# Two-block transformer kernel: paired value products, tanh gates, modulation chunks one a turn

## The chip, the cores and the metric

The kernel runs on one core of a Trainium2 chip, as one launch. The time is the device time of that core in microseconds (us). All of the work is in float32 or in pairs of rounded float32r parts. TensorE (PE) does the matrix products, VectorE (DVE) and ScalarE (ACT) the elementwise work, GpSimd (POOL) helps with weights, and SyncE (SP) issues the weight transfers.

## The reference

The reference is two transformer blocks after each other on 256 tokens of width 1024, each two layers deep. The change touches three places of it. In block one, attention is a mix of small attentions; the modulation rows of block two are computed beside it:

```
mod  = silu(c)     @ w_ada[l] + b_ada[l]
modc = silu(c_ctx) @ w_ada[l] + b_ada[l]        # 9 x 1024 values each
```

In block two, eight heads attend to 512 keys (256 context and 256 latent tokens), and three branches are merged through gates:

```
s = einsum('bqhd,bkhd->bhqk', q, k) * ATTN_SCALE
p = softmax(s, axis=-1)
o = einsum('bhqk,bkhd->bqhd', p, v)             # V_DIM = 64 a head
g = sigmoid(u @ w_bg + b_bg)                    # 3 x 1024 gates
y = (g0 * y_conv + g1 * y_mla + g2 * y_four) @ w_out
```

## The kernel before, in words

The program is written by hand: each engine has one instruction list, and the engines meet at semaphores. Nothing is reordered, so the order of the work is the order of the code.

**The weight stream.** All weights come as chunks of at most 128x1024 float32 (512 KB) through a ring of four slots. SP issues chunk n as soon as chunk n-4 has been used. For most products a chunk is split into a rounded high part (L771 on ACT) and the rest (L795 on DVE, L2361 and L2363 on POOL), and PE makes three passes (L834, L838, L841).

**Block one's attention** (`attention_pe`, `attention_act`, `attention_dve`) walks over 22 units a layer in 24 turns. In turn n PE does the scores of unit n+1 (L1100, L1108 or L1111, with masks at L1117), then the modulation chunks due in this turn (`ada_pe`, L932), then the transposes of unit n-1 (L1126 or L1129), then the values of unit n-2 (L1142, L1148), then a modulation fold if one is due (`ada_fold_pe`, L913). DVE takes the maximum (L1187), normalizes (L1210 to L1218) and adds the bias to folded rows (`ada_dve`, L953). ACT does the exponentials (L1240), the copies and the drain of the modulation bank (`ada_act`, L943). The first 11 units read 128 keys, the last 11 read 256.

**Modulation chunks.** `ADA_TICKS` says how many of a layer's 20 chunks are multiplied in each of 28 ticks; the first four ticks lie ahead of the attention, tick 4 + n is turn n. A chunk is two products of 32 output rows each; the chunks with an even number write rows 0 to 63 of the bank, the others rows 64 to 127. After 12 and after 20 chunks a bank is complete: ACT drains it one tick later, PE folds it two ticks later, DVE adds the bias three ticks later.

**Block two's attention** (`units_block2`) has in layer zero 16 units of one head with 512 keys and then 8 units of two heads with 256 keys; in layer one the 16 units of one head alone. In turn i PE does group i of the conv and fourier branch products (L834, L838, L841 for the gate, L2346, L2349, L2352 for the branch; turns 0 to 15 only), the scores of unit i+1 (L2003), the transposes of unit i-1 (L2012) and the values of unit i-2 (L2023). ACT does the exponential of unit i (L2055), the next weight split (L771), the gate (L2435), the copy of the transposes of unit i-1 (L2062) and the copy of the values of unit i-2 (L2067). The probabilities, `pt`, have two buffers by the parity of the unit. The value product of one head gives 64 of the 128 output rows of `bank7`: rows 0 to 63 for an even head, 64 to 127 for an odd one. A layer-zero branch turn of DVE also computes modulation rows (L962, L964).

**Tables.** The exponential of L2055 and the sigmoid of L2435 lie in different table sets of ScalarE, and an ACT_TABLE_LOAD stands ahead of each of them in turns 0 to 15; L2656 loads the sigmoid's set for the third branch.

## Time and profile before

| what | us |
|---|---|
| median of 3 runs | 2862.97 (2861.08 to 2864.32) |
| the profiled execution, its own time | 2866.21 |
| its span in the trace | 2864.4 |
| PE busy in the span | 2767.5 (97%) |
| DVE, ACT, POOL busy | 1779.1, 1124.7, 187.0 |

The trace is of one execution. Its own time is 1.8 us more than its span and 3.2 us more than the median. A busy engine here is one that has an instruction in flight; PE's instructions overlap, so the time of a row of PE work is best read from the start of one row to the start of the next.

### The profile page before, as it was taken

The page shows a single profiled execution, that of the slowest core. Times are in us where ns is not written, and L with a number is a line of the kernel's source. Part 1 is how long each engine was busy: PE and PEld are TensorE (multiplying, and loading weights), DVE is VectorE, ACT ScalarE, POOL GpSimd, SP SyncE. Part 2 cuts the span into 40 slices and gives each one's busy share as a digit, 9 for nine tenths or more (in the row PEclk, how much of TensorE's full clock was granted, in tenths as well). Part 3 has the DMA queues.
Part 4 walks back from the last instruction along what each step waited for, and adds up shares of the span by engine and source line. Part 5 has one row for each costly group of instructions (what it writes and reads, how often), then busy time and mean ns, then how long its engine had stood idle before and what let it go on. Part 6 is the DMA issues. An engine that isn't in the chain of part 4 may idle for free.

```text
span 2864.4 us, 45205 instructions
## 1 busy us (share of the span) xinstructions
PE 2767.5 (97%) x16512; PEld 2356.7 (82%) x16512; DVE 1779.1 (62%) x3034; ACT 1124.7 (39%) x1723; POOL 187.0 (7%) x184
## 2 busy tenths in 40 slices
PE   8999999989999999999999999999999999899998
PEld 7769999579988888775777788888788888689998
DVE  6467656576666565587665665555665557756665
ACT  5355444356442221335654232222322214584443
POOL 0000000000000000032223000000000000133000
PEclk9999999999999999999999999999999999999999
DMA  5535544625544443321332234443344433234454
GB/s 185 193 116 184 183 158 158 228 100 185 183 145 145 141 145 130 114 78 63 124 128 68 102 130 142 146 134 130 132 139 147 140 128 128 73 118 154 166 181 156
DMA packets 118650, 401.18 MB, mean 140 GB/s; under 512 B 12928, under 2 KB 20992, under 8 KB 118144
## 3 DMA queue, kind: packets, MB, share of 16 engines
q1 hardware_dynamic: 115408, 392.48, 40.5%
q10 hardware_dynamic: 3120, 7.07, 0.7%
q8 instruction: 77, 1.26, 0.2%
q14 instruction: 45, 0.37, 0.0%
HBM read 398.45 MB, written 1.05 MB: 139 GB/s over the span
## 4 chain that ended last, share of the span: by engine, by line
PE 86%; DVE 4%; issue 4%; ACT 2%; DMA 2%; POOL 1%; DVEq 1%; SPq 0%; ACTq 0%; POOLq 0%
PE bank L834 24%; PE bank L841 23%; PE bank L838 23%; PE bank L1570 2%; DMA ring<-weights 2%; PE bank L2023 1%; PE bank L2003 1%; PE bank L2352 1%; PE bank L2346 1%; PE bank L2349 1%; PE bank L1492 1%; DVE w_lo L795 1%; PE bank L1494 1%; POOL w_lo L795 1%; PE bank L1499 1%
## 5 line engine op out<-in xcount | busy, mean ns | idle before, releaser
L771 ACT ACTIVATE w_hi<-ring 128x1024 fp32r<-128x1024 f32 (+1 forms) x548 | 572.0, 1045 | 1179.3 <-DMA ring<-weights 1178.5
L795 DVE TENSOR_TENSOR w_lo<-ring,w_hi 128x1024 fp32r<-128x1024 f32 (+1 forms) x538 | 656.9, 1222 | 555.7 <-ACT w_hi L771 552.5
L838 PE MATMUL bank<-hn_hi,w_hi 128*128 128x256 f32 (+1 forms) x2816 | 882.8, 333 | 0.0
L841 PE MATMUL bank<-hn_lo,w_hi 128*128 128x256 f32 (+1 forms) x2816 | 882.7, 333 | 0.0
L841 PEld LDWEIGHTS bank<-hn_lo,w_hi 128*128 128x128 f32 x2816 | 534.9, 190 | 52.1
L838 PEld LDWEIGHTS bank<-hn_hi,w_hi 128*128 128x128 f32 x2816 | 534.7, 190 | 52.0
L834 PE MATMUL bank<-hn_hi,w_lo 128*128 128x256 f32 (+1 forms) x2816 | 547.0, 336 | 9.7 <-DVE w_lo L795 6.5
L834 PEld LDWEIGHTS bank<-hn_hi,w_lo 128*128 128x128 f32 x2816 | 439.9, 190 | 73.7 <-issue 14.4
L838 PE MATMUL bank<-hid_hi,w_hi 128*128 128x512 f32 (+1 forms) x704 | 248.7, 362 | 0.0
L841 PE MATMUL bank<-hid_lo_a,w_hi 128*128 128x512 f32 (+1 forms) x640 | 226.2, 362 | 0.0
L962 DVE SCALAR_TENSOR_TENSOR conds<-ring,con 128x1024 f32<-128x1024 f32 x106 | 130.9, 1235 | 53.5 <-DMA ring<-weights 37.1
L834 PE MATMUL bank<-hid_hi,w_lo 128*128 128x512 f32 (+1 forms) x704 | 156.4, 362 | 0.0
L838 PEld LDWEIGHTS bank<-hid_hi,w_hi 128*128 128x128 f32 x704 | 132.9, 189 | 20.5
L834 PEld LDWEIGHTS bank<-hid_hi,w_lo 128*128 128x128 f32 x704 | 121.9, 189 | 20.6
L841 PEld LDWEIGHTS bank<-hid_lo_a,w_hi 128*128 128x128 f32 x640 | 120.8, 189 | 18.7
L964 DVE SCALAR_TENSOR_TENSOR ring<-ring,con 128x1024 f32<-128x1024 f32 x106 | 131.6, 1241 | 0.0
L838 PE MATMUL bank<-up_hi,w_hi 128*128 128x256 f32 x512 | 125.6, 283 | 0.0
L841 PE MATMUL bank<-up_lo,w_hi 128*128 128x256 f32 x512 | 125.6, 283 | 0.0
L2698 DVE SCALAR_TENSOR_TENSOR hid<-work,par,hid 128x512 f32<-128x512 f32 (+1 forms) x180 | 117.4, 707 | 4.8
L2762 POOL MEMSET work<- 128x1716 f32 x2 | 3.1, 1528 | 1499.2 <-issue 790.0
L838 PEld LDWEIGHTS bank<-up_hi,w_hi 128*128 128x128 f32 x512 | 98.3, 192 | 0.0
L841 PEld LDWEIGHTS bank<-up_lo,w_hi 128*128 128x128 f32 x512 | 98.3, 192 | 0.0
(338 smaller groups left out, 3269.9 us busy)
## 6 DMA issues: line engine op xcount, KB each, us to landing
ring<-weights SPq DMA_DIRECT2D x694, 512.0 KB, 3.3
ring<-weights SPq DMA_DIRECT2D x32, 384.0 KB, 3.1
ring<-weights SPq DMA_DIRECT2D x32, 256.0 KB, 2.9
ring<-weights SPq DMA_DIRECT2D x28, 192.0 KB, 2.4
con<-consts ACTq DMA_DIRECT2D x1, 2063.0 KB, 9.7
con<-consts ACTq DMA_DIRECT2D x1, 1088.0 KB, 4.9
res<-ctx_cm ACTq DMA_DIRECT2D x1, 1024.0 KB, 5.8
con<-params ACTq DMA_DIRECT2D x1, 1024.0 KB, 7.0
```

Source lines behind the costliest of these rows:

```text
L771: act.activation(w_hi[:, slot, 0:w], ring[slot][:, 0:w], ACT.Copy).then_inc(s.w_hi, 1)
L795: eng.tensor_tensor(w_lo[slot][:, 0:w], ring[slot][:, 0:w], w_hi[:, slot, 0:w].bitcast(F32), ALU.subtract).then_inc(s.w_lo, 1)
L834: pe.matmul(dst, w_lo[slot][:, k * P:(k + 1) * P], x_hi(k), start=(start and k == order[0]), stop=False)
L838: pe.matmul(dst, high, x_hi(k), start=False, stop=False)
L841: return pe.matmul(dst, high, x_lo(k), start=False, stop=(stop and k == order[-1]))
L962: dve.scalar_tensor_tensor(out=conds[:, :], in0=ring[slot][:, :], scalar=1.0, in1=crow[:, 0:D], op0=ALU.mult, op1=ALU.mult, accum_out=to[: ...
L964: dve.scalar_tensor_tensor(out=ring[slot][:, :], in0=ring[slot][:, :], scalar=1.0, in1=crow[:, D:2 * D], op0=ALU.mult, op1=ALU.mult, accum ...
L1492: pe.matmul(dst[c], w_lo[slot[c]][:, k * P:(k + 1) * P], hn_hi[:, k, 0:w], start=(k == 0), stop=False)
L1494: pe.matmul(dst[c], w_hi[:, slot[c], k * P:(k + 1) * P], hn_hi[:, k, 0:w], start=False, stop=False)
L1499: mm = pe.matmul(dst[c], w_hi[:, slot[c], k * P:(k + 1) * P], hn_lo[:, k, 0:w], start=False, stop=(k == KT - 1))
L1570: mm = pe.matmul(bank[2 * parity(lin, g)][:, q], sq[:, k, q], ring[slot_of(lin, g, 0)][:, k * P:(k + 1) * P], start=(k == 0), stop=(k == K ...
L2698: last = dve.scalar_tensor_tensor(out=dst, in0=src, scalar=taps[:, m, k:k + 1], in1=dst, op0=ALU.mult, op1=ALU.add)
```

## The change

Three edits are made together.

1. **Two-head values.** The value products of two heads that follow each other (an even and an odd one) are done in the turn of the odd one, with the products of the two heads alternating. An even unit's turn has no value product and no copy of values; the odd unit's copy takes all 128 rows at once. The semaphores count two.
2. **Gates by the hyperbolic tangent.** sigmoid(x) becomes 0.5 tanh(x/2) + 0.5: a Tanh with scale 0.5 on a bias that DVE has halved, a drain of ACT, and an Identity with scale 0.5 and bias 0.5. The table set with exponential and tanh is loaded once ahead of the units; L2656 goes.
3. **Modulation chunks one a turn.** The 12 chunks of the attention's turns, which stood as 2, 2, 0, 4, 0, 0, 4 in turns 0 to 6, stand as one in each of turns 0 to 11. The first fold moves from turn 3 to turn 5, the second from turn 8 to turn 13.

```diff
-ADA_TICKS = ([2, 2, 2, 2, 2, 2, 0, 4, 0, 0, 4] + [0] * 17,) * 2
+ADA_TICKS = ([2] * 4 + [1] * 12 + [0] * 12,) * 2
...
+        def heads_of(units, n):
+
+            x = units[n]
+            if x.heads == 2:
+                return [(x, x.h, 0), (x, x.h + 1, 1)]
+            return [(units[n - 1], x.h - 1, 0), (x, x.h, 0)] if x.h % 2 else []
+
+        def latent_values(pe, units, n):
+            pair = heads_of(units, n)
+            if not pair:
+                return
+            x = units[n]
             pe.wait_ge(s.att_c, x.u + 1)
-            pe.wait_ge(s.att_o, x.o - 1 if x.heads == 1 else x.o)
+            pe.wait_ge(s.att_o, pair[0][0].o)
             kt = 4 // x.heads
-            for j in range(x.heads):
-                h = x.h + j
-                rows = slice((h % 2) * DH, (h % 2) * DH + DH)
-                for k in range(kt):
-                    mm = pe.matmul(bank[7][rows, 0:P], v2[:, x.key0 // P + k, h * DH:(h + 1) * DH],
-                                   pt[:, x.u % 2, (j * kt + k) * P:(j * kt + k + 1) * P],
+            for k in range(kt):
+                for j, (y, h, part) in enumerate(pair):
+                    mm = pe.matmul(bank[7][j * DH:(j + 1) * DH, 0:P], v2[:, y.key0 // P + k, h * DH:(h + 1) * DH],
+                                   pt[:, y.u % 2, (part * kt + k) * P:(part * kt + k + 1) * P],
                                    start=(k == 0), stop=(k == kt - 1), skip_group_check=True)
-            mm.then_inc(s.att_v, 1)
+            mm.then_inc(s.att_v, 1 if x.heads == 2 else 2)
...
+        def latent_out(act, units, n):
+            x = units[n]
+            if heads_of(units, n):
+                act.wait_ge(s.att_v, x.v + 1)
+                act.activation(att[:, x.h // 2, x.tt * P:(x.tt + 1) * P], bank[7][:, 0:P],
+                               ACT.Copy).then_inc(s.att_o, 1 if x.heads == 2 else 2)
...
-            act.activation(tmp2[:, parity(lin, g), 0:w], bank[2 * parity(lin, g) + 1][:, 0:w], ACT.Sigmoid,
-                           bias=bias[:, g.m + tile0, :]).then_inc(s.sig_g, 1)
+            gate = tmp2[:, parity(lin, g), 0:w]
+            act.activation(gate, bank[2 * parity(lin, g) + 1][:, 0:w], ACT.Tanh, scale=0.5,
+                           bias=bias[:, g.m + tile0, :])
+            act.drain()
+            act.activation(gate, gate, ACT.Identity, scale=0.5, bias=half_col).then_inc(s.sig_g, 1)
...
+            act.preload_act_table_set(EXP_TANH)
             for i in range(len(units) + 2):
...
-            act.preload_act_table(ACT.Sigmoid)
...
+            dve.tensor_scalar(param(f"bbg@@{l}"), param(f"bbg@@{l}"), 0.5, None, ALU.mult)
```

**PE, layer zero of block two, where the one-head units end and the two-head units begin.** bank4 and bank5 take scores, bank6 transposes, bank7 values; an x4 of L2023 is one head with 512 keys, or two heads with 256. Before:

```order
L2003 MATMUL bank4<-work_62,hid_61 128x256 x2
L2012 MATMUL bank6<-con0_71,work_62 128x128 x4
L2023 MATMUL bank7<-work_62 64x128 x4
L2003 MATMUL bank5<-work_62,hid_61 128x256 x2
L2012 MATMUL bank6<-con0_71,work_62 128x128 x4
L2023 MATMUL bank7<-work_62 64x128 x4
L2003 MATMUL bank4<-work_62,hid_61 128x256 x2
```

After, the same place (L2004, L2013 and L2033 are the same three steps):

```order
L2004 MATMUL bank5<-work_62,hid_61 128x256 x2
L2013 MATMUL bank6<-con0_71,work_62 128x128 x4
L2004 MATMUL bank4<-work_62,hid_61 128x256 x2
L2013 MATMUL bank6<-con0_71,work_62 128x128 x4
L2033 MATMUL bank7<-work_62 64x128 x8
```

Every second value step of a one-head unit is gone, and the other one has eight products instead of four.

**ACT, layer zero of block two, two turns in the middle of the conv branch.** work_62<-bank3 and bank1 with par12 are the gates. Before:

```order
L2055 ACT_TABLE_LOAD
L2055 ACTIVATE work_62,small_77<-bank4,small_77 128x512
L771 ACTIVATE w_hi_57<-ring2_51 128x1024
L2435 ACT_TABLE_LOAD
L2435 ACTIVATE work_62<-bank3,par12_74 128x512
L2062 ACTIVATE work_62<-bank6 128x512
L2067 ACTIVATE hid_61<-bank7 64x128
L2055 ACT_TABLE_LOAD
L2055 ACTIVATE work_62,small_77<-bank5,small_77 128x512
L771 ACTIVATE w_hi_57<-ring1_50 128x1024
```

After:

```order
L2065 ACTIVATE work_62,small_77<-bank4,small_77 128x512
L772 ACTIVATE w_hi_57<-ring2_51 128x1024
L2447 ACTIVATE work_62<-bank3,par12_74 128x512
L2450 ACTIVATE work_62<-work_62,small_77 128x512
L2072 ACTIVATE work_62<-bank6 128x512
L2065 ACTIVATE work_62,small_77<-bank5,small_77 128x512
L772 ACTIVATE w_hi_57<-ring1_50 128x1024
```

Both table loads of a turn are gone, one Identity (L2450) is new, and the copy of values stands in every second turn.

**PE, layer zero of block one, turns 0 to 2 of the attention.** L932 (L933 after) is a modulation chunk, L1111 (L1112) the scores, L1126 (L1127) the transposes. Before:

```order
L932 MATMUL bank1<-ring1_50,conds_76 32x512 x2
L932 MATMUL bank1<-ring2_51,conds_76 32x512 x2
L1111 MATMUL bank4<-hid_61 128x128
L1111 MATMUL bank5<-hid_61 128x128
L1117 MATMUL bank4<-mask_parts_79 128x128
L1117 MATMUL bank5<-mask_parts_79 128x128
L932 MATMUL bank1<-ring3_52,conds_76 32x512 x2
L932 MATMUL bank1<-ring0_49,conds_76 32x512 x2
L1126 MATMUL bank6<-con0_71,work_62 120x128
```

After:

```order
L933 MATMUL bank1<-ring1_50,conds_76 32x512 x2
L1112 MATMUL bank4<-hid_61 128x128
L1112 MATMUL bank5<-hid_61 128x128
L1118 MATMUL bank4<-mask_parts_79 128x128
L1118 MATMUL bank5<-mask_parts_79 128x128
L933 MATMUL bank1<-ring2_51,conds_76 32x512 x2
L1127 MATMUL bank6<-con0_71,work_62 120x128
```

A chunk stands alone between scores and transposes, where two or four stood together.

## Rows read from the trace of the kernel before

**Rows 1.** The page's part 1: busy us (share of the span) xinstructions, by engine.

```profile
PE 2767.5 (97%) x16512; PEld 2356.7 (82%) x16512; DVE 1779.1 (62%) x3034; ACT 1124.7 (39%) x1723; POOL 187.0 (7%) x184
```

**Rows 2.** Stretches: us, each engine's busy us, granted PE clock, DMA share, GB/s.

```profile
1341.00:1509.00 168.00, 167.13 (x760) 129.24 (x759) 105.48 (x167) 99.33 (x132) 46.57 (x46) 1.00 0.37 122
2484.00:2593.00 109.00, 109.00 (x765) 92.22 (x763) 54.78 (x105) 94.52 (x134) 40.53 (x49) 1.00 0.35 115
128.00:156.00 28.00, 21.12 (x130) 8.66 (x131) 14.74 (x57) 6.20 (x26) 0.95 (x1) 0.88 0.79 282
530.00:556.00 26.00, 19.99 (x119) 7.94 (x120) 14.63 (x54) 6.41 (x26) 0.00 (x0) 0.87 0.69 257
556.00:577.00 21.00, 20.34 (x156) 12.10 (x155) 11.61 (x62) 10.07 (x44) 0.00 (x0) 0.84 0.50 185
```

**Rows 3.** Timeline, PE, block two: start us, us, line, count [idle before <-releaser].

```profile
2533.09 1.09 PE L2023 MATMUL bank<-work 128*64 128x128 f32 x8
2534.11 1.21 PE L834 MATMUL bank<-hn_hi,w_lo 128*128 128x256 f32 x8
...
1518.04 0.66 PE L2023 MATMUL bank<-work 128*64 128x128 f32 x8
1518.64 1.13 PE L2003 MATMUL bank<-work,hid 96*128 96x256 f32 x4
```

**Rows 4.** Groups by line, 1345 to 1510 us: busy us, mean ns | idle before.

```profile
L2055 ACT ACT_TABLE_LOAD x16 | 20.5, 1283 | 0.3
L2435 ACT ACT_TABLE_LOAD x16 | 20.5, 1283 | 0.3
L2435 ACT ACTIVATE work<-bank,par 128x512 f32<-128x512 f32 x16 | 11.0, 690 | 5.8 <-PE bank L841 5.6
L2062 ACT ACTIVATE work<-bank 128x512 f32<-128x512 f32 x15 | 9.0, 598 | 41.8 <-PE bank L2012 41.8
```

**Rows 5.** Timeline, the end of layer one's units: ACT, DVE and PE.

```profile
2588.65 1.28 ACT L2055 ACT_TABLE_LOAD   x1
2589.95 0.69 ACT L2055 ACTIVATE work<-bank,small 128x512 f32<-128x512 f32 x1
...
2593.50 0.48 DVE L2452 SCALAR_TENSOR_TENSOR work<-bank,par,work 128x256 f32<-128x256 f32 x1 [0.56 <-ACT work L2435]
...
2595.18 0.66 PE L2012 MATMUL bank<-con,work 128*128 128x128 f32 x4 [0.90 <-DVE work L2045]
2595.77 1.84 PE L2023 MATMUL bank<-work 128*64 128x128 f32 x16
...
2602.41 0.86 PE L834 MATMUL bank<-hn_hi,w_lo 128*128 128x256 f32 x5 [0.30 <-DVE w_lo L795]
```

**Rows 6.** Timeline, PE, modulation chunks (four rows of L932 are one chunk).

```profile
142.55 1.92 PE L932 MATMUL bank<-ring,conds 128*32 128x512 f32 x4 [1.14 <-DMA ring<-weights]
...
151.24 1.05 PE L932 MATMUL bank<-ring,conds 128*32 128x512 f32 x4 [1.52 <-DMA ring<-weights]
...
126.58 1.06 PE L932 MATMUL bank<-ring,conds 128*32 128x512 f32 x8
...
159.44 1.92 PE L932 MATMUL bank<-ring,conds 128*32 128x512 f32 x16
...
547.18 1.05 PE L932 MATMUL bank<-ring,conds 128*32 128x512 f32 x4 [1.52 <-DMA ring<-weights]
548.44 1.76 PE L932 MATMUL bank<-ring,conds 128*32 128x512 f32 x4 [0.20 <-DMA ring<-weights]
```

**Rows 7.** Timeline, PE, starts of turns 0, 4 and 12, and a wait between.

```profile
139.71 0.50 PE L1111 MATMUL bank<-hid 64*128 64x128 f32 x4
...
154.46 1.06 PE L913 MATMUL bank<-con,work 128*128 128x6 f32 x8
155.44 0.49 PE L1111 MATMUL bank<-hid 64*128 64x128 f32 x4
...
157.85 0.33 PE L1129 MATMUL bank<-con,work 128*128 128x128 f32 x1 [0.45 <-DVE work L1218]
...
172.15 0.70 PE L1111 MATMUL bank<-hid 64*128 64x256 f32 x4
...
576.10 0.70 PE L1111 MATMUL bank<-hid 64*128 64x256 f32 x4
```

**Rows 8.** Timeline, DVE, turns 13 and 14 of layer zero.

```profile
177.12 0.61 DVE L1218 TENSOR_SCALAR work<-work,small 128x256 f32<-128x256 f32 x2
177.66 0.75 DVE L1187 TENSOR_REDUCE small<-bank 128x1 f32<-128x256 f32 x2
```

More of the change, by code:

```diff
@@ L40 @@
 LOG_EXP = "natural_log_exp_and_others"
+EXP_TANH = "exp_and_others"
 N_CMP = 15
@@ L608, in kernel_program @@
         conds = sb("conds", [P, D])
-        small = sb("small", [P, 404])
+        small = sb("small", [P, 405])
         sb("masks", [P, P])
@@ L676, in kernel_program @@
         (mx, negmx, smu, rcp, lb, lb_t, lb_u, gate_b, lf, lx, ly, lz, qkg, hk, hv, kcn, kcb, krot, c_max, c_sum, c_rcp,
-         eps_col, one_col) = carve(small, [4, 4, 4, 4, 4, 4, 4, 48, 8, 8, 8, 8, 10, 30, QH * N_CMP, 30, 30, 30, QH, QH,
-                                           QH, 1, 1])
+         eps_col, one_col, half_col) = carve(small, [4, 4, 4, 4, 4, 4, 4, 48, 8, 8, 8, 8, 10, 30, QH * N_CMP, 30, 30, 30, QH, QH,
+                                           QH, 1, 1, 1])
         gate = gate_b.rearrange("p (t c) -> p t c", t=TT)
@@ L2062, in latent_copy @@
             act.activation(pt[:, x.u % 2, :], bank[6][:, :], ACT.Copy).then_inc(s.att_c, 1)
-        def latent_out(act, x):
-            act.wait_ge(s.att_v, x.v + 1)
-            rows = slice((x.h % 2) * DH, (x.h % 2) * DH + DH) if x.heads == 1 else slice(0, P)
-            act.activation(att[rows, x.h // 2, x.tt * P:(x.tt + 1) * P], bank[7][rows, 0:P],
-                           ACT.Copy).then_inc(s.att_o, 1)
+        def latent_out(act, units, n):
[4 more added lines that the diff above has]
+                               ACT.Copy).then_inc(s.att_o, 1 if x.heads == 2 else 2)
         def gain_dve(dve, l, i):
@@ L2566, in block2_pe @@
                 if i >= 2:
-                    latent_values(pe, units[i - 2])
+                    latent_values(pe, units, i - 2)
             for g in turns(pe, PLAN["mrg_mla", l]):
@@ L2654, in block2_act @@
                 if i >= 2:
-                    latent_out(act, units[i - 2])
-            act.preload_act_table(ACT.Sigmoid)
+                    latent_out(act, units, i - 2)
             for g in turns(act, PLAN["mrg_mla", l], tail=2):
@@ L2845, in _ @@
             dve.memset(one_col, 1.0)
+            dve.memset(half_col, 0.5)
             dve.drain()
```

1 line of the change is left out of this document (removed).

## The prediction

> **What bounds the kernel now.** I read the busy shares first: PE is in use for 97% of the span [rows 1], so a microsecond counts only if it comes off PE's own list, or off a wait of PE. Then I read the two places that the edits touch. In block two's attention PE has no idle time at all: 167.13 of 168 us in layer zero, 109.00 of 109 us in layer one, at a granted clock of 1.00 [rows 2]. ACT is busy for 94.52 of those 109 us, so it is close behind. In block one's attention the first turns are different: PE is busy for 21.12 of 28 us and 19.99 of 26 us while the transfers run at 257 to 282 GB/s, and the granted clock is 0.88 and 0.87 [rows 2]. There PE waits for chunks.
>
> **The value products.** Each fp32 product is two rows of the trace, so L2023 x8 is one head with 512 keys. From its start to the start of the next step are 2534.11 - 2533.09 = 1.02 us [rows 3]. A two-head unit has the same eight rows, four for each half of the output rows, and takes 1518.64 - 1518.04 = 0.60 us [rows 3]. So products for different halves run side by side already: each half goes at its own pace of about 0.11 us a row (the step from four to eight rows in one half is 1.02 - 0.60 = 0.42 us). A pair of heads with 512 keys is eight rows in each half: 0.60 + 0.42 = 1.02 us, what one head costs now. The bound from the other side is 2.04 us, if the halves took turns; the two-head row is nearest and excludes it.
>
> There are 16 one-head units in each layer, 8 pairs. Layer zero: 8 x 1.02 = 8.2 us, all on a PE that never waits. Layer one: seven pairs give 7.1 us. The last pair gives nothing, because it now has to wait for the copy of the last transposes (0.60 us [rows 4] and some 0.15 us of signals), where the sixteen rows of before (1.84 us with the tail of the last one [rows 5]) filled that time with the other head: 0.75 + 1.09 = 1.84 us. Sum of the edit: **15.3 us**, bounds 14.3 and 16.3.
>
> The new wait: a `pt` buffer is free again only after the whole pair, so the ACT copy in a pair's turn comes after the value products, some 1.0 us later than now. Behind it in ACT's list stand the copy of values, the next exponential and the next weight split. In layer zero ACT waited 41.8 us for the transposes in 16 turns, 2.6 us a turn [rows 4], which covers it. In layer one it would not be covered without the second edit: ACT is busy for 94.52 of 109 us, and a turn would shrink by 0.51 us on average.
>
> **The gates.** A turn loses two table loads of 1.283 us each (32 in layer zero's window [rows 4], as many in layer one) and gains one Identity. Nothing of before shows that Identity; it reads and writes what the gate writes, 128x512, so I take the gate's 0.690 us in layer zero [rows 4], with a drain of 0.1 to 0.2 us. Net 2.57 - 0.8 = 1.8 us a turn off ACT, more in layer one where the tile is half as wide. That is cover and not time, since PE doesn't wait for ACT in these turns. The gate comes later by about 0.8 us than it would alone; DVE's merge waits for the branch product too (2 us after the gate product in layer zero), so it is hidden or late by 0.2 us off PE's path.
>
> Time comes back only at the end of layer one's units [rows 5]. PE waits 0.90 us for the last normalization, whose DVE work stands behind the merge, which waits for exponential, split, table and gate; with the tables gone the merge waits for the branch product alone and about half, 0.4 us, comes back. PE's wait of 0.30 us at 2602.41, behind the load of L2656, goes. Sum **0.7 us**, bounds 0 and 2. The halved bias is one small DVE instruction a layer: nothing.
>
> By the Trainium skill, "ScalarE: Activation LUTs", section "What ACT_TABLE_LOAD costs", a switch costs 1283 ns and a drain of 1380 ns more. The load here is 1.28 us, and the exponential behind it begins 1.30 us after it (2588.65 to 2589.95 [rows 5]), so the trace agrees with the first figure and shows no drain after it. By the page's sum ACT's list in a layer-one turn would be 2 x 1.38 = 2.8 us longer than it is seen to be, longer than PE's turn, and the table loads would be the bound there; the rows decide against that.
>
> **The modulation chunks.** A chunk alone takes 1.05 us, two together 1.06, four 1.92 [rows 6]: two neighbours write different rows of the bank and run side by side. So two chunks cost 0.93 us of PE to the start of the next step, and one alone also costs 0.93; with the signals between, 1.02. Spreading twelve chunks over twelve turns costs 12 x 1.02 = 12.2 us a layer, where layer zero now spends 11.9 (blocks of 4.0, 1.2, 4.8 and 1.9 us, of which 1.14 and 1.52 us are visible waits for chunks [rows 6]). By that the edit gives nothing. It gives what the chunks now hide. I walk through the turns.
>
> Layer zero: turn 0 starts at 139.71 and turn 4 at 155.44 [rows 7]. With one chunk a turn, turn 0 ends at 141.3; turn 1 still waits for its chunk until 142.5 (that landing doesn't depend on the change [rows 6]) and ends at 143.75; turns 2 and 3 need 2.1 and 2.7 us: 148.5. Turns 4 to 11 take 16.71 us now (to 172.15 [rows 7]); without the block of four (1.86), without the two waits for DVE that a chunk fills (0.45 [rows 7] and 0.21), with 8 x 1.02 us of chunks: 22.35 us, to 170.85. One fold leaves this stretch and one comes in. Gain 1.3 us. Layer one: the chunk that comes at 547.18 [rows 6] still comes then, turn 4 starts at 551.15, turn 12 at 573.5 instead of 576.10 [rows 7]: 2.6 us, part of it the 0.84 clock of that stretch [rows 2]. Against that, the second fold (0.98 us, 154.46 to 155.44 [rows 7]) with its ACT copy and four DVE additions now stands in turn 13, where DVE goes without a pause from normalization to the next maximum (177.12, 177.66 [rows 8]): I charge 1.1 us a layer. Sum 3.9 - 2.2 = **1.7 us**. Bounds: -6 if the waits for chunks return in every layer beside 12 lone chunks, +8 if the chunks find more idle time than the two waits counted.
>
> **The sum.** 15.3 + 0.7 + 1.7 = 17.7 us. The profiled execution took 2866.21 us; it becomes 2848.5. It lies 3.2 us above the median of the runs, so the median becomes 2845.3: I say **2845.5**.
>
> **The rivals.**
>
> *ACT sets the pace (chance 0.12).* Copy, values copy, exponential, split, tanh and Identity now follow the end of the pair, and if this list is longer than PE's turn, about half of the first edit is lost: 15.3 / 2 = 8, time 2853. Against it: the ACT list of a layer-one turn is 94.52 / 16 = 5.9 us now, and about 4 without tables, under a PE turn of 5.4 at least. The Trainium skill, "TensorEngine Tiling (Array Packing)", section "Performance Considerations", warns that tiling speeds up TensorE but not the emptying of PSUM, so that the copy may become the bottleneck; here the pair is emptied by one copy where two stood.
>
> *The spread is worth more (0.15).* PE's clock stays at its full level in both layers' first turns (0.88, 0.87, 0.84 now) and waits for DVE are filled in more turns: 5 us a layer instead of 0.85, time 2837.
>
> *The spread costs (0.06).* Landings stay late and lone chunks add up: -3 us a layer, 2845.5 + 1.7 + 6 = 2853.
>
> *The heads don't run side by side (0.02).* If alternating products of two accumulations take turns, a pair takes 2.04 us and the change doesn't do what it says: 2861, no change.
>
> *Slower (0.03).* A chunk alone at the half clock takes 1.76 us against 1.05 at the full one (548.44 and 547.18 [rows 6]), 0.7 more, and the rest of such a turn some 0.5 more. If twelve thin turns in each layer kept PE at 1.2 GHz, 24 x 1.2 = 29 us would be lost against 17.7 gained: 2874. It decides from about 15 low turns of 24. Against it: the denser stretch from 156 us has a PE nearly always busy.
>
> The forecast itself has 0.62, with a range of its own of 2840 to 2851.
>
> **How the numbers follow.** To reach 8 in 10 the range takes in the forecast, the richer spread at 2837 and the two losses at 2853: 2836 to 2855. A measurement tells this kernel from no change from about 0.2%, 5.7 us. Faster than 2857: 0.62 + 0.12 + 0.15 + 0.06 = 0.95, of which I give 0.01 to the case in which two losses meet: 0.94. Within 0.2%: 0.03. Slower: 0.03.
>
> **What would show it.** In the profile after: the paired value step at 1.0 us with x16 rows, half as many steps; PE without waits in block two's attention, layer zero's part shorter by 8 us and layer one's by 7; no table load between the units; chunk rows of 1.05 us, one in each of turns 0 to 11; turn 12 of block one earlier by 1 to 3 us. The forecast is wrong if the paired step takes 2 us, if PE waits for the ACT copy in the pair's turn, or if lone chunks are seen at the half clock for many turns.

## The result and the profile after

| | median us | runs | lowest to highest | ratio to before (95% interval) |
|---|---|---|---|---|
| before | 2862.02 | 4 | 2854.75 to 2864.32 | |
| changed | 2839.25 | 4 | 2838.28 to 2842.64 | 0.9928 (0.9916 to 0.994) |
| changed, on a second chip | 2840.44 | 5 | 2838.65 to 2841.81 | 0.9934 (0.992 to 0.9947) |

The kernel is faster by 0.7%, about 20 us, by both ratios; the forecast was 2845.5 with a range of 2836 to 2855. The profiled execution took 2842.64 us (span 2840.7), 23.6 us less than that of before.

The page's part 1 of the changed kernel, which answers to [rows 1]. ACT is 59 us less busy, PE 17 us.

```profile
PE 2750.5 (97%) x16512; PEld 2340.8 (82%) x16512; DVE 1782.5 (63%) x3037; ACT 1065.5 (38%) x1690; POOL 193.3 (7%) x184
```

The same stretches as in [rows 2] (us, then each engine's busy us, granted clock, DMA share, GB/s): block two's attention in layer zero and layer one, then block one's first turns in layer zero and in layer one (two).

```profile
1334.00:1493.00 159.00, 158.18 (x749) 122.60 (x748) 108.23 (x166) 67.95 (x110) 44.07 (x45) 1.00 0.39 129
2468.00:2569.00 101.00, 100.58 (x756) 86.01 (x755) 57.13 (x104) 59.88 (x112) 46.09 (x48) 1.00 0.39 124
126.00:154.00 28.00, 24.04 (x149) 10.59 (x151) 17.56 (x72) 8.31 (x35) 0.95 (x1) 0.88 0.75 258
527.00:553.00 26.00, 21.16 (x133) 8.87 (x133) 17.34 (x68) 8.45 (x34) 0.00 (x0) 0.93 0.75 262
553.00:574.00 21.00, 20.45 (x152) 10.66 (x150) 11.71 (x56) 9.83 (x42) 0.00 (x0) 1.00 0.56 181
```

PE is as dense as before in block two, and ACT has fallen from 94.52 to 59.88 us in layer one's stretch. Now the paired step, in the timeline of PE (start, us, engine, line, count), which answers to [rows 3]: an even unit's turn without a value step, then an odd one's with the pair (L2013 transposes, L2033 values, L835 gate products, L2357 branch products).

```profile
1382.24 0.62 PE L2357 MATMUL bank<-means_r,w_lo 128*128 128x512 f32 x2
...
1385.15 0.60 PE L2013 MATMUL bank<-con,work 128*128 128x128 f32 x4
1385.50 2.09 PE L835 MATMUL bank<-hn_hi,w_lo 128*128 128x512 f32 x8
...
1391.07 0.61 PE L2357 MATMUL bank<-means_r,w_lo 128*128 128x512 f32 x2
...
1393.97 0.60 PE L2013 MATMUL bank<-con,work 128*128 128x128 f32 x4
1394.50 1.09 PE L2033 MATMUL bank<-work 128*64 128x128 f32 x16
1395.53 1.66 PE L835 MATMUL bank<-hn_hi,w_lo 128*128 128x512 f32 x6
```

The pair takes 1395.53 - 1394.50 = 1.03 us, as forecast. But from the start of the transposes to the next step it is 0.35 us where gate products follow and 0.53 us where a value step follows, so a value step that goes takes 0.18 us more with it. The even turn shows the sum: in the kernel before it was 10.03 us long, after it is 1391.07 - 1382.24 = 8.83 us, 1.20 us less. The rows of before:

```profile
1390.40 0.62 PE L2346 MATMUL bank<-means_r,w_lo 128*128 128x512 f32 x2
...
1400.43 0.62 PE L2346 MATMUL bank<-means_r,w_lo 128*128 128x512 f32 x2
```

PE's modulation chunks (L933) and turn 12's start (L1112 at 169.37), which answer to [rows 6, 7]:

```profile
139.10 1.05 PE L933 MATMUL bank<-ring,conds 128*32 128x512 f32 x4 [0.64 <-DMA ring<-weights]
...
155.80 0.28 PE L1118 MATMUL bank<-mask_parts 128*128 128x128 bf16 x2
156.02 1.05 PE L933 MATMUL bank<-ring,conds 128*32 128x512 f32 x4
157.00 0.44 PE L1130 MATMUL bank<-con,work 128*128 128x128 f32 x2
...
169.37 0.70 PE L1112 MATMUL bank<-hid 64*128 64x256 f32 x4
```

From a lone chunk's start to the next step it is 0.98 us, and from the masks into the chunk 0.22 us. The waits for landings have become fewer: in the profile of before PE waited 2.9 us for them in layer zero's first turns and 2.5 us in layer one's, in this one 1.1 and 0.5 us, and in the second profile of the changed kernel (below) not at all in either layer. The waits for L1218's normalization fell from 1.8 us in each layer to 0.6 and 1.2 us in that second profile. And the end of layer one's units, which answers to [rows 5]:

```profile
2571.21 0.63 PE L2013 MATMUL bank<-con,work 128*128 128x128 f32 x4 [0.85 <-ACT work L2072]
2572.53 1.09 PE L2033 MATMUL bank<-work 128*64 128x128 f32 x16 [0.69 <-ACT work L2072]
```

From the last transposes to the gate products behind the units it was 2.36 us before (2595.18 to 2597.54) and is 2.34 us now (2571.21 to 2573.55): the last pair gives nothing, as forecast.

**Lengths of four stages.** The table has all profiled executions. A stage runs from the start of one row on PE to the start of another. Block one's stages begin with the first bias product (L1607 before) and end with the first product behind the attention (L1044). Block two's begin with the first scores (L2003) and end with the first branch product behind the units (L2346). These lengths don't contain the rest of the program, where the granted clock differs from run to run by chance; within them it can differ too. Each row is one execution.

| us | block one, l. 0 | block one, l. 1 | block two, l. 0 | block two, l. 1 |
|---|---|---|---|---|
| before | 96.65 | 98.34 | 192.34 | 109.50 |
| pair alone | 95.69 | 96.29 | 184.30 | 102.26 |
| tanh alone | 96.56 | 95.48 | 191.69 | 110.12 |
| pair and tanh | 97.86 | 96.00 | 182.54 | 101.09 |
| spread alone | 98.06 | 95.17 | 192.37 | 109.50 |
| changed | 95.93 | 95.06 | 183.27 | 101.74 |
| changed again | 94.94 | 94.38 | 182.61 | 101.09 |
| waits kept | 95.62 | 95.01 | 182.97 | 101.29 |
| head by head | 95.53 | 95.81 | 186.68 | 104.97 |
| full width | 94.75 | 94.54 | 187.45 | 106.73 |
| two, alternate turns | 92.53 | 94.56 | 183.25 | 101.10 |
| two, from turn 2 | 93.29 | 91.76 | 183.04 | 101.10 |
| the same again | 93.68 | 93.29 | 183.17 | 101.09 |
| the same, values first | 93.51 | 93.30 | 186.61 | 100.96 |

### The profile page after: what moved, and what is told of

It reads as the page before. It is cut to its first block, busy times and chain, and to the rows that moved or that the text cites. A ratio compares the mean times of both kernels' runs of the same rounds, so it can differ in the third digit from the quotient of the medians.

```text
span 2840.7 us, 45223 instructions
## 1 busy us (share of the span) xinstructions
PE 2750.5 (97%) x16512; PEld 2340.8 (82%) x16512; DVE 1782.5 (63%) x3037; ACT 1065.5 (38%) x1690; POOL 193.3 (7%) x184
## 4 chain that ended last, share of the span: by engine, by line
PE 85%; DVE 5%; issue 4%; DMA 2%; ACT 2%; POOL 1%; DVEq 1%; ACTq 0%; SPq 0%; POOLq 0%
PE bank L835 24%; PE bank L842 23%; PE bank L839 23%; PE bank L1571 2%; DMA ring<-weights 2%; PE bank L2004 1%; DVE w_lo L796 1%; PE bank L2363 1%; PE bank L2357 1%; PE bank L2360 1%; DVE work L2125 1%; DVE hn_lo L1056 1%; PE bank L933 1%; POOL w_lo L796 1%; PE bank L1493 1%
## 5 line engine op out<-in xcount | busy, mean ns | idle before, releaser
L835 PE MATMUL bank<-hn_hi,w_lo 128*128 128x256 f32 (+1 forms) x2816 | 546.6, 336 | 9.5 <-DVE w_lo L796 6.4
L835 PEld LDWEIGHTS bank<-hn_hi,w_lo 128*128 128x128 f32 x2816 | 440.3, 190 | 70.7 <-issue 12.4
L835 PE MATMUL bank<-hid_hi,w_lo 128*128 128x512 f32 (+1 forms) x704 | 156.4, 362 | 0.0
L835 PEld LDWEIGHTS bank<-hid_hi,w_lo 128*128 128x128 f32 x704 | 121.9, 189 | 20.6
## 6 DMA issues: line engine op xcount, KB each, us to landing
ring<-weights SPq DMA_DIRECT2D x28, 192.0 KB, 2.3
```

The costliest lines, as they stand in the source:

```text
L835: pe.matmul(dst, w_lo[slot][:, k * P:(k + 1) * P], x_hi(k), start=(start and k == order[0]), stop=False)
```

## The experiments

**The pair alone.** The first edit of the change, with the sigmoid's gates and the old `ADA_TICKS`.

> Only the paired value products; the sigmoid gates with their table loads and the old places of the modulation chunks stay. In the trace of the changed kernel each pair of heads takes 1.20 us off PE's list in block two's attention, not 1.02: the value step that goes takes its gap at the semaphore (about 0.18 us) with it. Theory 'the whole step goes': 8 pairs in layer zero and 7 in layer one at 1.20 us, 18 us, minus up to 1 us at the end of layer one's units: 2845 us, ratio 0.994. Theory 'the tanh is the cover' : with 94.5 of 109 us of ACT busy in layer one before, its shorter PE turn leaves ACT too little room, PE waits for the copy of the transposes or for the gate's bank, and layer one gives only half: 8 x 1.20 + 4 = 13.6 us, 2849 us, with waits of PE for ACT in layer one's turns that are not there in the changed kernel. Theory 'as predicted': 15.3 us, 2847.5 us.

Measured: 2844.28 us (5 runs), ratio 0.995 (0.9937 to 0.9964). In layer zero's steady part every pair of turns is 1.20 us shorter, and in layer one's four of seven, though both table loads are still in every turn; layer one's first three pairs give 1.13, 1.08 and 1.09 us. The stretches of steady turns in its trace:

```profile
1336.00:1488.00 152.00, 151.16 (x727) 118.40 (x726) 104.84 (x163) 90.15 (x119) 45.17 (x44) 1.00 0.39 131
2466.00:2566.00 100.00, 100.00 (x751) 85.62 (x750) 54.24 (x103) 90.64 (x126) 39.60 (x48) 1.00 0.39 123
```

In layer one ACT is busy for 90.64 of 100 us and PE shows no idle time. So ACT doesn't set the pace, with or without the tanh. It does hold PE a little in layer one's first three short turns, by about 0.1 us each, which the busy time of PE doesn't show, since the products ahead are still in flight. There the gate products start 0.44 us behind the transposes instead of 0.35, just after DVE has finished the weight split, which had waited for ACT's half of it:

```profile
2487.40 1.23 DVE L796 TENSOR_TENSOR w_lo<-ring,w_hi 128x1024 fp32r<-128x1024 f32 x1 [2.17 <-ACT w_hi L772]
...
2488.34 0.60 PE L2013 MATMUL bank<-con,work 128*128 128x128 f32 x4
2488.78 0.47 PE L835 MATMUL bank<-hn_hi,w_lo 128*128 128x256 f32 x2
```

Most of the loss is at two places: where layer zero goes over to two-head units, and at the end of layer one. PE and, between, ACT:

```profile
1495.07 0.66 PE L2013 MATMUL bank<-con,work 128*128 128x128 f32 x4 [0.81 <-DVE work L2055]
1496.73 1.13 PE L2004 MATMUL bank<-work,hid 96*128 96x256 f32 x4 [1.01 <-ACT work L2065]
...
1494.36 1.28 ACT L2065 ACT_TABLE_LOAD   x1
1495.66 0.47 ACT L2065 ACTIVATE work<-bank,small 128x256 f32<-128x256 f32 x1
...
2569.51 0.66 PE L2013 MATMUL bank<-con,work 128*128 128x128 f32 x4 [1.70 <-DVE work L2055]
2570.85 1.09 PE L2033 MATMUL bank<-work 128*64 128x128 f32 x16 [0.69 <-ACT work L2072]
```

The copies come after the pair, at the seam the exponential's table load after them, and the scores wait for the exponential. The theory that the whole step goes is confirmed in nearly all turns, and the cover theory holds at the ends and for 0.3 us in layer one's turns: 15 pairs at 1.20 us are 18.0 us, and the two stages give 8.04 + 7.24 = 15.3 us.

**The tanh alone.**

> Only the gates by tanh; values head by head and chunks in their old places. Theory 'cover, not time': ACT loses about 60 us of busy time in the two layers (two table loads of 1.28 us a turn less, one Identity of 0.5 to 0.7 us more), PE's turns stay as they are, and 0 to 1 us comes off at the end of layer one's units: 2861 to 2863 us, ratio 0.9995. Rival 'the loads were in the way': if the table loads delayed the weight split or the copy by enough to hold PE, layer one's 16 turns get shorter: 2 us or more, under 2860.5 us.

Measured: 2861.46 us (11 runs), ratio 1.0005 (0.9996 to 1.0014): nothing. Layer zero's units are 0.65 us shorter. Layer one's are 0.62 us longer, and 0.65 us of that is a landing at their start (a PE wait for `w_lo`, 0.4 us), which the profile of the changed kernel has too and its second profile has not. At layer one's end, PE and DVE:

```profile
2584.45 0.66 PE L2013 MATMUL bank<-con,work 128*128 128x128 f32 x4 [0.87 <-DVE work L2046]
...
2582.24 0.48 DVE L2456 SCALAR_TENSOR_TENSOR work<-bank,par,work 128x256 f32<-128x256 f32 x1 [0.65 <-PE bank L2353]
```

The wait of 0.90 us [rows 5] is still 0.87. The merge waited for the gate before; it now waits for the branch product, and it does come earlier: it starts 0.40 us after the start of the last branch product (2581.84 to 2582.24), where it was 0.96 us before (2592.54 to 2593.50). But the addition behind it took 0.97 us instead of 0.43, and the 0.56 us were gone. The addition before, then the addition and POOL's subtraction with the tanh alone:

```profile
2594.06 0.43 DVE L2458 TENSOR_TENSOR work<-work 128x256 f32<-128x256 f32 x1
```

```profile
2582.76 0.73 POOL L2375 TENSOR_TENSOR hid_hi<-hid,hid_hi 128x256 fp32r<-128x256 f32 x1 [0.16 <-issue]
2582.79 0.97 DVE L2462 TENSOR_TENSOR work<-work 128x256 f32<-128x256 f32 x1
```

In the kernel before, the addition came when that subtraction was nearly over (2593.45, 0.73 us long). All traces here agree: in layer one's units this addition takes 0.43 us in every turn in which POOL has no such instruction under way, and where it starts with 0.19 us or more of one left it ends 0.28 us behind POOL's (1.00 us with 0.72 us left, 0.73 with 0.45, 0.48 with 0.19). No run moves POOL's work alone, so the cause is read from the traces and not tested.

**The spread alone.**

> Only the twelve modulation chunks of block one's attention, one in each of turns 0 to 11; block two as before. In the trace of the changed kernel layer zero's attention is 1.4 us shorter and layer one's 3.9 us, and layer one kept the granted clock at 1.00 where it had been 0.84. Theory 'the spread gives the waits and the clock': 4 to 6 us, 2857 to 2859 us, and the same two figures by layer. Rival 'layer one's gain is the clock's chance': the clock falls again in layer one here and the layer gives about 1 us, 2860.5 us. Rival of the prediction (1.7 us): 2861.3 us.

Measured: 2855.25 us (11 runs), ratio 0.9988 (0.9979 to 0.9997), 3.4 us; the interval, 0.9 to 6.0 us, leaves both the 4 us of the first theory and the 1.7 us of the prediction standing. The gain goes with the clock: the mean granted clock of these runs is 0.9901, that of before beside them 0.9882, and at about 1.5 us for each 0.001 (last section) that is some 2.9 of the 3.7 us between the two means. Layer one gives 3.2 us against the profile of before, layer zero loses 1.4. Neither is the spread's own: layer one in the pair alone, the tanh alone and both together, with the old ticks, is 2.0 to 2.9 us shorter than in the profile of before too, and layer zero of the spread alone holds a stretch of 6.8 us at the lower clock, 13 us into the stage, where before had one of 3.4 us. From the attention's first scores on, the changed kernel's layer one was 3.9 us shorter than in that profile. The three kernels with the old ticks have the same instructions there as before, and between 556 and 566 us they gain 3.06 us. In the profile of before PE's clock stood at its lower level for part of the stretch below; in those three it didn't, nor in the spread alone (1.00 from 553 to 574 us).

```profile
558.00:568.00 10.00, 9.54 (x60) 4.36 (x58) 4.25 (x24) 4.03 (x19) 0.00 (x0) 0.66 0.61 220
```

So the trace of one execution misled in both directions, and the means over the table are the better measure: block one's two stages are 96.69 + 96.53 us over four kernels with the old ticks, 95.81 + 95.00 over six with one chunk a turn. That is 2.4 us, and rough: the sums of single kernels run from 192.0 to 195.0 us with the old ticks and from 189.3 to 193.2 with one chunk a turn.

**Pair and tanh.**

> Pair and tanh together, chunks in their old places: what the changed kernel is without the third edit. Theory 'each edit stands alone': the first two give 9.1 + 7.8 = 17 us, 2846 us, and the step from here to the changed kernel (2839.25) is the spread's 5 to 6 us. Theory 'tanh is the cover of the pair': this kernel is 3 us or more faster than the sum of the pair alone and the tanh alone. Theory 'as predicted': 16.0 us, 2847 us.

Measured: 2843.14 us (5 runs), ratio 0.9948 (0.9934 to 0.9961). Block two's stages are 9.80 + 8.41 = 18.2 us shorter than before, 2.9 us more than with the pair alone, where the tanh alone gave 0.65. The place is the one that the pair alone lost; PE at the seam of layer zero, without a wait:

```profile
1499.10 0.66 PE L2013 MATMUL bank<-con,work 128*128 128x128 f32 x4
1499.79 1.13 PE L2004 MATMUL bank<-work,hid 96*128 96x256 f32 x4
```

In layer one it is 8.41 = 7 x 1.20: the last pair gives nothing, as forecast. The theory that the tanh is the pair's cover asked for 3 us or more beyond the sum of both alone; the stages show 2.3 us. The timed runs don't show it: their mean is 2844.06 us against 2844.33 with the pair alone. With five runs each, spread over 6 us, they don't rule it out either.

**Two chunks in every second turn.**

```diff
-ADA_TICKS = ([2] * 4 + [1] * 12 + [0] * 12,) * 2
+ADA_TICKS = ([2] * 4 + [2, 0] * 6 + [0] * 12,) * 2
```

> The changed kernel with two modulation chunks in every second turn of block one's attention (turns 0, 2, 4, 6, 8, 10) and none between, instead of one in each of turns 0 to 11. Theory 'a lone chunk costs as much PE time as two neighbours' (0.93 us to the next step): six chunk stretches of 0.93 us a layer fall away; where PE does not wait, 5.6 us a layer, 11 us for both, 2828 us. Theory 'the lone chunks stand in idle time': in turns 4 to 11 PE waits for DVE where no chunk stands, and the chunks have to wait for their landings in turns 0 to 3; half of it or less comes back: 2836 us. Rival 'the landings decide': two chunks in turn 0 need the second landing, PE waits there as in the kernel before, and the kernel is as fast as the changed one, 2839.5 us.

Measured: 2837.34 us (5 runs), ratio 0.9919 (0.9905 to 0.9932); the changed kernel beside it 2840.44. On PE, a turn with two chunks, a turn with none, and the wait that appears:

```profile
151.96 0.29 PE L1118 MATMUL bank<-mask_parts 128*128 128x128 bf16 x2
152.17 1.06 PE L933 MATMUL bank<-ring,conds 128*32 128x512 f32 x8
153.17 0.44 PE L1130 MATMUL bank<-con,work 128*128 128x128 f32 x2
...
154.33 0.28 PE L1118 MATMUL bank<-mask_parts 128*128 128x128 bf16 x2
154.45 0.39 PE L1130 MATMUL bank<-con,work 128*128 128x128 f32 x2
...
166.78 0.33 PE L1127 MATMUL bank<-con,work 128*120 128x128 f32 x1 [1.31 <-DVE work L1208]
```

From masks to transposes are 1.21 us with two chunks, 1.20 with one (rows above) and 0.12 with none. The steps to the next start differ by 1.08 us, so six times that a layer was to be had; against the means with one chunk a turn the stages are 3.3 and 0.4 us shorter. A wait of 1.31 us for DVE has come back where no chunk fills it, in each layer, and so has a second stretch at the lower clock, 42 us into the stage in both layers. The theory of 2836 us, that half of it or less comes back, is met.

**The same from turn 2 on**, run twice.

```diff
-ADA_TICKS = ([2] * 4 + [1] * 12 + [0] * 12,) * 2
+ADA_TICKS = ([2] * 4 + [0, 0] + [2, 0] * 6 + [0] * 10,) * 2
```

> As the run with two chunks in every second turn, but from turn 2 on (turns 2, 4, ..., 12). The chunks have landed by then, so that no wait for a landing is left in turns 0 and 1; but SP issues nothing new while four slots are full, and the weight stream stands still for two turns longer. Theory 'the waits for landings are what is left': faster than the run that starts in turn 0 by 1 to 2 us a layer. Rival 'the stream must not stand still': the same wait comes back in turns 4 to 8, when the later chunks are not there, and the time is that of the other run or worse, 2836 to 2842 us.

> The run with two chunks in every second turn from turn 2 on, once more on whatever chip this is, to see whether its gain over the changed kernel holds. Theory 'six stretches of a lone chunk less a layer' (1.08 us each, of which waits for DVE take half back): ratio to the kernel before 0.9915, 4 us under the changed kernel's 0.993. Rival 'chance of the clock in the first look': ratio 0.993.

Measured: 2836.07 us, ratio 0.9919 (0.9905 to 0.9932), and the second time 2837.03 us, ratio 0.9908 (0.9891 to 0.9925), 5 runs each. It is about 4 us faster than the changed kernel by the medians; the ratio of the second run, 0.9908, is nearer to the 0.9915 of its theory than to the rival's 0.993. It is not shown to be faster than the run that starts in turn 0: the ratio is the same, 0.9919, and block one's stages are 187.1 us there. With the values-first run, which has the same chunks, block one's stages are 186.3 us against 190.8 with one chunk a turn. In both profiles of this kernel PE waits for no landing in the attention, so the rival on the weight stream falls; but the 1 to 2 us a layer that the first theory expected don't show either. The clock takes part of the gain back: in all eight layers with two chunks in every second turn it fell to its lower level once more behind the first turns, and the mean granted clock is 0.986 to 0.987 against 0.988 for the changed kernel. What is left are waits for DVE and one for ACT. Some of PE's waits in layer zero from 120 to 190 us (total, times, longest) in the second of these runs:

```profile
PE bank L1127 <- DVE work L1208: 1.6, 2, 1.3
PE bank L1112 <- ACT work L1236: 0.9, 1, 0.9
```

**The changed kernel again.**

> The changed kernel without any edit, beside the others on one chip, to see how much of a difference between two profiled executions is its own granted clock. Over the runs so far a run's time goes down by about 1.36 us for each 0.001 of mean granted clock. Theory 'part of the 23.7 us between the two profiled executions was the clock': with the clock taken out the changed kernel is 18 to 19 us under the kernel before (2841 against 2860 us at 0.988). Rival 'the whole 23.7 us is the change': 23 us under it at equal clock.

Measured: 2840.44 us against 2859.64 before. Its mean is 2840.2 at a mean granted clock of 0.9884, that of before 2858.7 at 0.9882: 18.4 us at nearly equal clock, as the first theory says. Of the 23.6 us between the two first profiles some 5.7 are not the change's: 2.6 us in the program's first 45 us, which the change doesn't touch, and the 3.06 us above. The 3.06 us are the clock. Of the 2.6 us about 1.1 are (the clock stood at its lower level for 6.8 us there before and for 3.4 us after); the rest are waits that ended earlier.

**The waits kept.** The even unit's turn waits on the same semaphores and multiplies nothing.

```diff
             if not pair:
+                pe.wait_ge(s.att_c, x.u + 1)
+                pe.wait_ge(s.att_o, x.o - 1)
                 return
```

> The changed kernel with the two semaphore waits of the value step kept in the even unit's turn, where no product stands. In the changed kernel the transposes are followed by the gate products after 0.35 us, and before a value step it is 0.53 us; a pair gives 1.20 us where 1.02 was forecast. Theory 'the 0.18 us are the waits themselves': they come back, a pair gives 1.02 us, layer zero's units are 1.4 us longer and layer one's 1.3 us. Theory 'the 0.18 us belong to the products' (another shape of weights behind the transposes): satisfied waits cost nothing, and a pair still gives 1.20 us.

```profile
1383.84 0.60 PE L2013 MATMUL bank<-con,work 128*128 128x128 f32 x4
1384.20 2.09 PE L835 MATMUL bank<-hn_hi,w_lo 128*128 128x512 f32 x8
```

One execution took 2841.24 us. From the transposes' start to the gate products it is 0.36 us, and a pair still gives 1.20 us: a satisfied wait costs 0.01 us at most here, and the 0.18 us belong to the products. The expectation ahead of the pair alone, which called them a gap at the semaphore, was wrong.

**Head by head.** The pair's loops are exchanged: four products of the even head, then four of the odd one.

```diff
-            for k in range(kt):
-                for j, (y, h, part) in enumerate(pair):
+            for j, (y, h, part) in enumerate(pair):
+                for k in range(kt):
```

> The changed kernel with the pair's products head after head (four of the even head, then four of the odd one) in one value step, instead of alternating. Theory 'the halves run side by side whatever the order' (the two-head units of the kernel before issued theirs head after head and took 0.60 us for eight rows): the step stays at 1.03 us and a pair at 1.20 us. Rival 'the order matters': four products of one half stand behind each other before the other half begins, the step takes up to 1.03 + 0.42 = 1.45 us or more, and each pair gives 0.8 us or less.

```profile
1395.19 1.58 PE L2033 MATMUL bank<-work 128*64 128x128 f32 x16
1396.70 2.11 PE L835 MATMUL bank<-hn_hi,w_lo 128*128 128x512 f32 x8
```

One execution took 2848.88 us. The step is 1.51 us instead of 1.03, in every pair; block two's stages are 4.1 and 3.9 us longer than in the second profile of the changed kernel. The order matters: without the alternation 0.49 of 1.20 us a pair is lost. The Trainium skill, "TensorE: Matmul & The Clock Gate", section "Packing small matmuls — row/col tiling", says that matmuls start and end strictly in program order. By that rule the odd head's first row would start behind the even head's last, which starts 0.82 us into the step, and the step would take 0.82 + 1.02 = 1.84 us, as an estimate. The trace doesn't agree: for 0.49 us the rows start one by one, 0.11 us apart behind the first, the pace of one half, and from the fifth row on they start in twos.

The second series must be the odd head's, since rows of one half come 0.11 us apart, though it is issued behind all eight rows of the even one, and 0.49 + 1.02 = 1.51 us. When it starts, three rows of the even head have not started. In the two-head units of before, also issued head after head, the second row starts 0.02 us after the first and the step takes 0.60 us: there too three rows of the first head were still ahead. So both fit one reading, that a product can begin while up to three rows of the other half ahead of it have not started; no run tests it further.

**Values first**, with the chunks of the run from turn 2 on.

```diff
+                if i >= 2:
+                    latent_values(pe, units, i - 2)
                 if 1 <= i <= len(units):
                     latent_turn(pe, units[i - 1])
-                if i >= 2:
-                    latent_values(pe, units, i - 2)
```

> The changed kernel with chunks as in the run with two from turn 2 on, and in block two with the value products ahead of the turn's transposes instead of behind them. The start of a value step comes 0.18 us later behind the transposes than the gate products do. Theory 'the 0.18 us stand behind transposes alone': with the values behind the scores the gap goes in every second turn, 15 x 0.18 = 2.7 us off the two layers, 2833 us. Rival 'the gap belongs to the change of shape and moves with the value step': it appears ahead of the value step or behind it, and block two stays at 183 and 101 us. Rival 'the copy comes later and PE waits for it': block two gets longer by some us at the layers' ends, 2838 us.

Measured: 2839.05 us (5 runs), ratio 0.9925 (0.9912 to 0.9939). PE, scores, values, transposes, gate products:

```profile
1391.19 1.02 PE L2004 MATMUL bank<-work,hid 96*128 96x512 f32 x2
1392.15 1.09 PE L2033 MATMUL bank<-work 128*64 128x128 f32 x16
1393.17 0.66 PE L2013 MATMUL bank<-con,work 128*128 128x128 f32 x4
1393.59 2.09 PE L835 MATMUL bank<-hn_hi,w_lo 128*128 128x512 f32 x8
```

The gap moved with the value step: the scores now take 0.96 us to the next step (0.86 before transposes), the transposes 0.42 (0.35). A pair gains 0.03 us instead of 0.18. Layer zero's 186.61 us hold a stretch at the lower clock (6.8 us from 1512.6 us on, at the seam), so they don't tell what the edit costs there. This version is not worth having.

**Full width.** Each value product of the one-head units over all 128 rows; those units' attention values are changed by it.

```diff
+                    mm = pe.matmul(bank[7][:, 0:P], v2[:, y.key0 // P + k, cols],
+                                   pt[:, y.u % 2, (part * kt + k) * P:(part * kt + k + 1) * P],
+                                   start=(k == 0 and j == 0), stop=(k == kt - 1 and j == 1),
+                                   skip_group_check=True)
```

> The changed kernel with each value product of the one-head units taken over all 128 output rows (128 weight columns, both heads' values) instead of 64. Both heads' products are added into the same rows, so the attention's values of the one-head units are not those of the reference: this part of the computation is changed, only the time of the step counts. Theory 'the 0.18 us are the change between full-width and half-width products': the value step now starts 0.35 us behind the transposes, like the gate products, instead of 0.53. Rival 'the 0.18 us come from something else in the value step' (its accumulation, its operands' buffers): 0.53 us stays. The step itself: products of one accumulation over the same rows go one after the other, eight of them where four and four stood side by side; by the step from four to eight rows in one half (0.42 us for two products) the eight take 1.02 + 4 x 0.21 = 1.9 us instead of 1.03 us, and each of the 16 pairs costs 0.7 us more, 2851 us.

```profile
1391.30 0.60 PE L2013 MATMUL bank<-con,work 128*128 128x128 f32 x4
1391.74 1.95 PE L2035 MATMUL bank<-work 128*128 128x128 f32 x16
1393.45 2.09 PE L835 MATMUL bank<-hn_hi,w_lo 128*128 128x512 f32 x8
```

One execution took 2847.68 us. The gap is 0.44 us, halfway: about half of the 0.18 us goes with the change between full and half width, the other half stays. The step is 1.71 us, not the 1.9 us that was expected, so running side by side saves 0.68 us a pair. The way back from half width has a price too: from the start of the last value row to the start of the gate products it is 0.20 us in the changed kernel (1395.33 to 1395.53) and 0.03 us here (1393.42 to 1393.45), and that is inside the 1.03 us. The Trainium skill, "TensorEngine Tiling (Array Packing)", section "Tiling Modes", says that changing the tiling mode drains TensorE. The gaps agree with that for half of the 0.18 us ahead of the value step and for the way back; what the other half of the 0.18 us is stays open.

## Why the prediction was right, and where its steps were not

**The value products (15.3 us forecast).** The reading was right: two halves run side by side, a pair costs what one head cost (1.03 us against 1.02), PE has no idle time there, the last pair of layer one gives nothing. The term was mis-sized: "8 x 1.02" counted from the value step's start to the next step, and left out that the step ahead of it also gets shorter. A step that goes is worth 1.20 us, the 0.18 us ahead of it included. 15 such pairs are 18.0 us, and the pair with the tanh gives 18.2 (9.80 + 8.41). The bounds of 14.3 to 16.3 don't hold it; that the pair alone gave just 15.3 is luck, 18.0 less 2.7 us lost elsewhere, 2.4 of them at the seam and at the end of layer one. The prediction read the price of a step from its own two rows; the price of taking it away is the difference of two whole turns.

**The copy behind the pair.** "In layer one it would not be covered without the second edit" was wrong but for 0.3 us: with ACT busy for 90.64 of 100 us four of layer one's seven pairs of turns still got 1.20 us shorter and the other three 1.08 to 1.13, where the prediction feared half of the edit. It was right in another place, at the seam of layer zero and the end of layer one: together with 0.3 us in the turns, 2.3 us more came from having both edits, by the stages. The prediction didn't look at the seam at all.

**The gates (0.7 us).** The size was about right and the place wrong: the 0.65 us of the stages are at layer zero's seam, which isn't in the sum. Of the 0.90 us wait 0.03 came back, not 0.4. The step that failed is the one from an earlier merge to an earlier normalization: the merge came 0.56 us earlier, but the DVE addition between them took 0.54 us longer beside POOL. The 0.30 us at 2602.41 [rows 5] are gone, and 0.16 to 0.20 us of wait stand one group later. The timed runs of the tanh alone can't show 0.7 us: 1.0005 (0.9996 to 1.0014).

The sum by the Trainium skill, "ScalarE: Activation LUTs", with a drain of 1380 ns behind each load, is decided against by the pair alone: 2.8 us more in each layer-one turn would have had PE waiting, and PE was busy for 100.00 of 100 us.

**The modulation chunks (1.7 us).** The sum was about right: 2.4 us by the stages, 3.4 (0.9 to 6.0) by the timed runs. How much of it is the waits that went and how much the clock stays open; the timed runs put most on the clock. The charge of 1.1 us a layer for the second fold was never measured by itself. A lone chunk costs 1.08 us, not 1.02, and turn 12 starts at 169.37 instead of 170.85, mostly because this execution was 2.0 us early at the attention's start. The rival in which the clock stays full is partly true: PE's clock stood at its lower level at some time later than 10 us into block one's stage in 4 of 8 layers with the old ticks, in 1 of 12 with one chunk a turn, and in 8 of 8 with two in every second turn. Why it fell in the ones and not in the others is not shown. The price of 5 us a layer was too high: the dip between 558 and 568 us cost 3.06 us.

**The median.** Forecast 2845.5, measured 2839.25 and 2840.44: the kernel is 5 to 6 us faster than forecast. Of these 2.7 are the pairs and 0.7 the chunks, by the stages; the rest lies within what runs of one kernel differ by. The range holds both, but partly through a rival: the forecast's own range was 2840 to 2851, and 2839.25 lies nearer to the 2837 us of the richer spread, whose reason (5 us a layer from the chunks) is not what the runs showed. The prediction also took 3.2 us off for the profiled execution, rightly: 5.7 us of that profile's distance to the changed kernel's have nothing to do with the change.

## What to carry to other kernels

Price a step that is removed by the whole turn with it and without it, not from its own start to the next: the change of shape around it has a price too. Don't take a busy share of 100% as proof that an engine was never held: compare the lengths of the same turn in two kernels. Interleave products for different halves of the output rows; one half after the other loses much of the overlap. When small fillers share the array, put two neighbours together and leave turns without any, and look whether the gain comes back as a wait for another engine. Before explaining a difference of a few microseconds between two traces, compare the granted clock in the same stretch, or the same stretch in a third kernel.

## What the runs showed of the hardware

- 16 rows for two halves took 1.03 us alternating and 1.51 us one half after the other; eight products over all rows took 1.71 us. Two-head units with two products for each half had taken 0.60 us one half after the other [rows 3] and take 0.59 us alternating in the changed kernel (1504.09 to 1504.68), so with two products a half the order costs nothing.
- Two waits on semaphores already reached cost PE 0.01 us at most (0.36 against 0.35 us).
- ACT at 91% busy, with two table loads of 1.28 us in each turn, held PE for about 0.1 us in each of three turns in 100 us, and PE was still counted as busy for all of them.
- A DVE addition of 128x256 float32 took 0.43 us alone. Where a POOL subtraction was under way at its start it ended 0.28 us behind that one, 0.97 us in all in the tanh alone.
- From the last row of one step to the first of the next PE took 0.03 us where both were full width (transposes to gate products), 0.20 us from full-width transposes to half-width value products, and 0.20 us from those back to full-width gate products.
- Over all timed runs, compared within one kernel, a run's time fell by about 1.5 us for each 0.001 of its mean granted clock.
